# The chunk matrices of a delta-rule recurrence: X read off XT by 128x128 transpositions and half-switching copies, where a third product per chunk made it

## The chip, the cores and the metric

The kernel runs on one core of one Trainium2 chip. The metric is the device time of one execution in microseconds: 4751.49 us is the median of three runs of the kernel before (4750.6 to 4759.0). PE is the matrix engine (TensorE), PEld its weight loads, DVE is VectorE, ACT is ScalarE, POOL is GpSimd, SP issues DMAs.

## What is computed

One launch computes three blocks of two layers each on a sequence of 512 tokens, 1024 wide, in fp32. The change lies in the odd layer of the third block, whose branch C is a recurrence in two directions over 16 heads of width 64:

```python
def wkv7_step(state, inp):
    r, w, k, v, a, b = inp
    sa = jnp.einsum('...ij,...j->...i', state, a)
    state = (state * w[..., None, :] + sa[..., :, None] * b[..., None, :]
             + v[..., :, None] * k[..., None, :])
    y = jnp.einsum('...ij,...j->...i', state, r)
    return state, y
```

with a = -kk and b = kk * a' (kk is the l2-normalised key, a' a gate), r, k, v, w the receptance, key, value and decay. The state of a head is 64x64.

## The kernel before

The function `wkv` (L3398) works in chunks of 64 tokens. A chunk needs the inverse of a unit triangular 64x64 matrix made of products of the a's and b's. X holds that inverse, XT its transpose. They begin as the identity with the first off-diagonal entries put in (L3887 for XT, L3890 for X), and five levels double the size of the diagonal blocks that are inverted (2, 4, 8, 16, 32, then 64 wide). Only XT is needed at the end (`XTC`).

There are 16 steps: 8 pairs of heads times 2 directions (d). A pair of heads lies on the two halves of the 128 partitions, so `heads` (L3524) issues each product twice, 64x64 on the upper and on the lower half; the 8 chunks of the sequence lie side by side in the free dimension. Each fp32 matmul of the code shows as two matmul rows and two weight loads in the trace. Chunks 0 to 3 are half "a" of a level, 4 to 7 half "b".

A level l (L3666 to L3696 on PE) is:
- POOL: C = AS times the mask of the level (L3508), once `t` of the level before is done.
- PE: t = C and XT, per chunk, 16 matmuls, halves a and b (L3673), into bank 0 and 1.
- ACT: T1 = copy of t, half by half (L3783).
- PE: ct = X and T1, 16 matmuls (L3685), into banks 4 and 5. It waits for X of the level before and for T1.
- PE: cx = T1 and X, 16 matmuls (L3694), into banks 2 and 3; not in level 5.
- DVE: XT += ct, half by half (L3906), then X += cx, half by half (L3911).

Beside the matrices of step n, the kernel runs the chain of step p = n - 1: the state passes through the 8 chunks in order, and each level carries one link of it, between t, ct and cx on PE: `ch_g` (8 matmuls, the first four make G), DVE's copy of G (`gk`, L3798), `ch_sa` (2 matmuls), ACT's copy of SA (`san`, L3720), `ch_ys` (8 matmuls), DVE's scaling of the state (`upd`, L3805). Links 0 to 2 stand in the first part of a step, links 3 to 7 in levels 1 to 5. The first step has no chain beside it, and after the last step a chain runs alone.

The order on each engine is the order in which the code is written; nothing schedules it. `rounds` (L3455) writes out the first two and the last three turns and puts the others in a loop of three passes with four steps each. Engines wait on counting semaphores: a `Marks` object gives each engine's steps names ("t1a", "xt1b", "x1a") in the order in which it completes them, and `count(n, name)` is the value to wait for. `K.apart` is a semaphore increment that keeps the waits before and after it apart.

Of the kernel before, what the change touches and what calls it, by code (L numbers as in the profile page):

```python
# [15 lines left out]
P = 128  # L16
# [3381 lines left out]
def wkv(K, base, WDA, W2, RZ, out):  # L3398
# [24 lines left out]
    AS, X, XT, T1, C = (chunks(a) for a in (L, EP, EN, RN, TMP))  # L3423
# [5 lines left out]
    hr = lambda h: slice(64 * h, 64 * h + 64)  # L3429
# [3 lines left out]
    def halves(b):  # L3433

        two = K.psflat[:, b * 512:b * 512 + 1024].rearrange("p (b n) -> p b n", b=2)[:, :, 0:256]
        return two.rearrange("p b (j t) -> p b j t", t=64)
    block_of = lambda b, j: halves(b)[:, j // 4, j % 4, :]
    couple = lambda b: K.psflat[:, b * 512:b * 512 + 1024].rearrange("p (j m t) -> p j m t", m=2, t=64)
    chunks_of = lambda half: range(4) if half == "a" else range(4, 8)
    in_half = lambda a, half: a[:, 0:4, :] if half == "a" else a[:, 4:8, :]  # L3440
    bank_half = lambda b, half: halves(b)[:, "ab".index(half), :, :]
    levels = range(1, 6)

    PM = Marks(K, "wkv_pe", "wa kkn tv tb bon tk sa srb sk " +
               " ".join(f"t{l}a t{l}b ct{l}a ct{l}b" + (f" cx{l}a cx{l}b" if l < 5 else "") for l in levels))
    AM = Marks(K, "wkv_act", "sw aa sqk ln rn ep en eplus ee vt bt kt as " + " ".join(f"t{l}a t{l}b" for l in levels))
    DM = Marks(K, "wkv_dve", "r k v lw scan lprev max kk b bhat a1 kp rk ahat khat rhat bo bo2 xt0 x0 mrb mak mrk " +
               " ".join(f"xt{l}a xt{l}b" + (f" x{l}a x{l}b" if l < 5 else "") for l in levels))
    GM = Marks(K, "wkv_pool", "w2f pr pk pv ix ixt " + " ".join(f"c{l}" for l in levels))

    def chunk(d, j):
# [21 lines left out]
    with nc.Block() as block:  # L3473
# [38 lines left out]
        def _(pe):  # L3512
# [11 lines left out]
            def heads(dst, lhsT, rhs, start=True, stop=True):  # L3524

                for h in range(2):
                    mm = pe.matmul(dst[hr(h)], lhsT[hr(h)], rhs[hr(h)], start=start, stop=stop, skip_group_check=True)  # L3527
                return mm
# [4 lines left out]
            def ch_g(p, pd, j):  # L3533
                if p is None:
                    return
                m = chunk(pd, j)
                if j == 0:
                    pe.wait_ge(DM.sem, DM.count(p, "xt5b"))
                    pe.wait_ge(K.sem("y_sum"), K.count("y_sum", p))
                    K.apart(pe)  # L3540
                    heads(GP, MAK[:, pd, m, :], VT[:, pd, m, :]).then_inc(K.sem("ch_g"), 1)
                else:
                    pe.wait_ge(K.sem("ch_s"), K.count("ch_s", 7 * p + j))
                    K.apart(pe)
                    heads(GP, MAK[:, pd, m, :], VT[:, pd, m, :], stop=False)
                    heads(GP, AR[:, pd, m, 0, :], S, start=False).then_inc(K.sem("ch_g"), 1)
                heads(yp(m), VT[:, pd, m, :], MRK[:, pd, m, :], stop=False)
                if j:
                    heads(yp(m), S, AR[:, pd, m, 1, :], start=False, stop=False)
# [32 lines left out]
            def step(n, d, c, par, p, pd, nth, fin=None):  # L3582
                def projection(half):
                    if nth is None:
                        return
                    q = 1 - par
                    if d == 0 and half == 0:
                        pe.wait_ge(K.landed[(first + q) % 2], 16 * ((first + q) // 2 + 1) + 16 * nth)
                    m = 2 * d + half
                    pe.wait_ge(K.sem("raw_kept"), K.count("raw_kept", 4 * (c + 1) + m - 1))  # L3590
                    pe.wait_ge(DM.sem, DM.count(n - 1, "x4b"))
                    project(q, m)
                if n is not None:
                    pe.wait_ge(GM.sem, GM.count(n, "w2f"))
# [71 lines left out]
                for l in levels:  # L3666
                    if n is not None:
                        pe.wait_ge(GM.sem, GM.count(n, f"c{l}"))
                        for half in "ab":
                            pe.wait_ge(DM.sem, DM.count(n, f"xt{l - 1}{half}" if l > 1 else "x0"))  # L3670
                            K.apart(pe)
                            for j in chunks_of(half):
                                mm = heads(block_of(0, j), C[:, j, :], XT[:, j, :])  # L3673
                            mm.then_inc(PM.step(f"t{l}{half}"), 1)
                    ch_g(p, pd, l + 2)
                    if n is not None:
                        if l == 1:
                            pe.wait_ge(DM.sem, DM.count(n, "mrb"))
                        else:
                            pe.wait_ge(DM.sem, DM.count(n, f"x{l - 1}b"))  # L3680
                        for half in "ab":
                            pe.wait_ge(AM.sem, AM.count(n, f"t{l}{half}"))
                            K.apart(pe)
                            for j in chunks_of(half):
                                mm = heads(block_of(4, j), X[:, j, :], T1[:, j, :])  # L3685
                            mm.then_inc(PM.step(f"ct{l}{half}"), 1)
                    ch_sa(p, pd, l + 2)
                    if n is not None and l < 5:
                        if l == 1:
                            pe.wait_ge(DM.sem, DM.count(n, "mrk"))  # L3690
                            K.apart(pe)
                        for half in "ab":
                            for j in chunks_of(half):
                                mm = heads(block_of(2, j), T1[:, j, :], X[:, j, :])  # L3694
                            mm.then_inc(PM.step(f"cx{l}{half}"), 1)
                    ch_ys(p, pd, l + 2)  # L3696


# [93 lines left out]
        def _(dve):  # L3792
# [31 lines left out]
            def step(n, d, c, par, p, pd, nth, fin=None):  # L3824
# [73 lines left out]
                for l in levels:  # L3898
                    gk(p, pd, l + 2)
                    if n is not None:  # L3900
                        last = f"x{l - 1}b" if l > 1 else "x0"
                        dve.wait_ge(DM.sem, DM.count(n, last))
                        for half in "ab":
                            dve.wait_ge(PM.sem, PM.count(n, f"ct{l}{half}"))
                            x = in_half(XT, half)
                            dve.tensor_tensor(x if l < 5 else in_half(XTC[:, d], half), x, bank_half(4, half), ALU.add)\  # L3906
                               .then_inc(DM.step(f"xt{l}{half}"), 1)
                        for half in "ab" if l < 5 else "":
                            dve.wait_ge(PM.sem, PM.count(n, f"cx{l}{half}"))
                            x = in_half(X, half)  # L3910
                            dve.tensor_tensor(x, x, bank_half(2, half), ALU.add).then_inc(DM.step(f"x{l}{half}"), 1)  # L3911
                    upd(p, pd, l + 2)
                if p is not None:
                    dve.wait_ge(K.sem("ch_ys"), K.count("ch_ys", 8 * p + 8))
# [185 lines left out]
```

## Time and profile before

| | us |
|---|---|
| median of three runs | 4751.49 |
| the profiled execution | 4748.9 |
| its span, first to last instruction | 4746.7 |
| PE busy | 4400.7 (93%) |
| PE weight loads busy | 3338.7 (70%) |
| DVE busy | 2457.6 (52%) |
| ACT busy | 1608.9 (34%) |
| POOL busy | 320.5 (7%) |

The `wkv` function takes from about 3808 to 4650 us of the span. The mean granted clock of PE is 0.960 of full speed. A span is counted from the first instruction, a row's start from the same point. In a timeline row "x128" means that many instructions merged, and the duration is that of the merged run; PE's ends are modelled. The bracket behind a row gives the engine's idle time before it, and what ended it; "issue" stands for nothing that the profile shows.

### The profile page before, as it was taken

How to read it: one execution, taken by the hardware profiler on the slowest of the kernel's cores; microseconds unless marked ns; L12 is line 12 of the kernel's file. 1: busy time of each engine (PE TensorE's matmuls, PEld its weight loads, DVE VectorE, ACT ScalarE, POOL GpSimd, SP SyncE). 2: the span in 40 equal slices, each digit the busy share in tenths (PEclk: the TensorE clock that was granted, in tenths of full speed). 3: DMA queues.
4: the chain of work that ended last, by engine and by line, in shares of the span. 5: the costliest groups of instructions: out<-in, count | busy, mean ns of one | idle time of the engine just before them, and what ended most of it. 6: DMA issues, size and time to landing. Idle time of an engine off the chain costs nothing. (4 is left out here: it accounts for less than half of the span.)

```text
span 4746.7 us, 79005 instructions
## 1 busy us (share of the span) xinstructions
PE 4400.7 (93%) x32172; PEld 3338.7 (70%) x32172; DVE 2457.6 (52%) x3963; ACT 1608.9 (34%) x2467; POOL 320.5 (7%) x307
## 2 busy tenths in 40 slices
PE   8898999899999989999998899978998999999987
PEld 7665788676688767888887644456877567766775
DVE  3634543433445331777777379943534355555553
ACT  2324322323322232666665210133222233334332
POOL 0120000000000000111111000000000022221220
PEclk9888999998999999999999999989998999999998
DMA  3201222221122232111111312111221210000101
GB/s 146 108 19 71 89 89 107 76 89 71 57 104 89 110 129 82 56 59 51 59 54 35 142 53 89 71 54 71 107 98 71 105 37 20 21 20 20 56 3 54
DMA packets 36644, 337.23 MB, mean 71 GB/s; under 512 B 4080, under 2 KB 6384, under 8 KB 18544
## 3 DMA queue, kind: packets, MB, share of 16 engines
q1 hardware_dynamic: 36336, 332.76, 19.0%
q8 instruction: 238, 3.90, 0.3%
q14 instruction: 70, 0.57, 0.0%
HBM read 320.16 MB, written 12.58 MB: 70 GB/s over the span
## 5 line engine op out<-in xcount | busy, mean ns | idle before, releaser
L539 PE MATMUL ps<-hi,weight_parts 128*128 128x512 f32 x5136 | 1611.5, 395 | 120.6 <-DVE lo L406 75.7
L539 PEld LDWEIGHTS ps<-hi,weight_parts 128*128 128x128 f32 x5136 | 979.8, 191 | 340.8 <-issue 122.0
L539 PE MATMUL ps<-lo,weight_parts 128*128 128x512 f32 x2568 | 1011.7, 394 | 0.0
L527 DVE TENSOR_TENSOR weight_parts<-w,weight_parts 128x1024 fp32r<-128x1024 f32 (+1 forms) x336 | 406.8, 1212 | 967.6 <-ACT weight_parts L518 967.5
L518 ACT ACTIVATE weight_parts<-w 128x1024 fp32r<-128x1024 f32 (+1 forms) x336 | 351.7, 1048 | 1197.0 <-PE ps L539 996.1
L539 PEld LDWEIGHTS ps<-lo,weight_parts 128*128 128x128 f32 x2568 | 490.5, 191 | 102.0
L3527 PEld LDWEIGHTS ps<-buffers 64*64 64x64 f32 x12544 | 430.5, 136 | 125.9 <-issue 123.9
L3527 PE MATMUL ps<-buffers 64*64 64x64 f32 x12544 | 460.0, 226 | 52.0 <-issue 27.1
L2409 PE MATMUL ps<-x_parts,column_parts 128*128 128x512 f32 x1536 | 360.7, 392 | 10.5 <-DVE column_parts L2643 9.9
L2884 PE MATMUL ps<-x,w 128*128 128x512 f32 x768 | 331.6, 595 | 6.8 <-PEq L815 6.8
L2409 PEld LDWEIGHTS ps<-x_parts,column_parts 128*128 128x128 f32 x1536 | 286.5, 189 | 69.9 <-DVE column_parts L2643 10.3
L2947 DVE SCALAR_TENSOR_TENSOR buffers<-buffers,vecs 128x392 f32<-128x392 f32 (+14 forms) x480 | 286.8, 678 | 0.0
L2884 PEld LDWEIGHTS ps<-x,w 128*128 128x128 f32 x768 | 146.5, 191 | 191.2 <-issue 191.2
L3520 PE MATMUL ps<-h,w 128*128 128x512 f32 x512 | 228.7, 601 | 1.2 <-PEq L3351 1.2
L3520 PEld LDWEIGHTS ps<-h,w 128*128 128x128 f32 x512 | 96.3, 192 | 117.3 <-issue 115.8
L2434 PE MATMUL ps<-h 128*128 128x128 f32 x1024 | 129.4, 281 | 35.0 <-DVE w L2687 22.3
L2434 PEld LDWEIGHTS ps<-h 128*128 128x128 f32 x1024 | 124.5, 195 | 42.3 <-DVE w L2687 21.9
L3783 ACT ACTIVATE buffers<-ps 128x256 f32<-128x256 f32 x160 | 61.3, 383 | 174.7 <-PE ps L3527 168.9
L3508 POOL TENSOR_TENSOR buffers<-buffers,const 128x512 f32<-128x512 f32 x80 | 101.6, 1270 | 272.2 <-PE ps L3527 200.3
L2643 DVE TENSOR_TENSOR column_parts<-w,column_parts 128x1024 fp32r<-128x1024 f32 x64 | 78.5, 1228 | 58.1 <-ACT column_parts L2515 58.1
L2623 POOL MEMSET w<- 128x1024 f32 x1 | 1.0, 951 | 1542.4 <-POOLq L2130 1542.4
L2409 PE MATMUL ps<-context_parts,column_parts 128*128 128x256 f32 x768 | 104.0, 292 | 0.0
(481 smaller groups left out, 5337.1 us busy)
## 6 DMA issues: line engine op xcount, KB each, us to landing
w<-in_weights SPq DMA_DIRECT2D x126, 2048.0 KB, 7.9
w<-in_wh SPq DMA_DIRECT2D x64, 512.0 KB, 3.6
v_kept<-buffers SPq DMA_DIRECT2D x4, 1024.0 KB, 5.2
buffers<-v_kept SPq DMA_DIRECT2D x16, 256.0 KB, 2.6
h<-x_kept SPq DMA_DIRECT2D x2, 2048.0 KB, 10.5
x<-in_xT SPq DMA_DIRECT2D x4, 512.0 KB, 10.7
x_kept<-h SPq DMA_DIRECT2D x1, 2048.0 KB, 7.0
vc_kept<-x SPq DMA_DIRECT2D x4, 512.0 KB, 2.6
```

What stands on the lines that cost most here:

```text
L518: act.activation(K.parts[:, j % 2, 0, 0:nk, :], part_of(K, slot, j, nk, by_row), ACT.Copy)\
L527: dve.tensor_tensor(K.parts[:, j % 2, 1, 0:nk, :], part_of(K, slot, j, nk, by_row), K.parts[:, j % 2, 0, 0:nk, :].bitcast(F32), ALU.subtra ...
L539: mm = pe.matmul(ps, K.parts[:, j % 2, m, k, :], x[:, k * T:(k + 1) * T], start=(first and k == 0 and n == 0), stop=(last and k == nk - 1 ...
L2409: mm = pe.matmul(o, parts[:, half, w, k, :], src[:, m, k, 0:width], start=(k == 0 and n == 0), stop=(k == 7 and n == 2), skip_group_check= ...
L2434: mm = pe.matmul(bank[:, s], l[:, s], r[:, s], start=True, stop=True)
L2643: dve.tensor_tensor(half[:, 1], weight(name), half[:, 0].bitcast(F32), ALU.subtract).then_inc(DL.step(name), 1)
L2884: mm = pe.matmul(bank(i, j), w[:, k, j * P:(j + 1) * P], K.H[:, k, :], start=(k == 0), stop=(k == 7))
L2947: dve.scalar_tensor_tensor(y, u, w, y, ALU.mult, ALU.add).then_inc(K.sem("tapped"), 1)
L3508: pool.tensor_tensor(C, AS, on_chunks(f"{'clow' if d == 0 else 'cup'}{l}"), ALU.mult).then_inc(GM.step(f"c{l}"), 1)
L3520: mm = pe.matmul(K.ps[:, 2 + m % 2, :], w[:, k, m * P:(m + 1) * P], K.H[:, k, :], start=(k == 0), stop=(k == 7))
L3527: mm = pe.matmul(dst[hr(h)], lhsT[hr(h)], rhs[hr(h)], start=start, stop=stop, skip_group_check=True)
L3783: act.activation(in_half(T1, half), bank_half(0, half), ACT.Copy)\
```

## The change

X of a level is no longer made by the third product and the add. From level 2 on, once t is issued, PE transposes XT as it stands after the level before: four transpositions of 128x128, each over two neighbouring chunks, into banks 2 and 3. What comes out has the head in the free dimension and the chunk's parity on the halves of the partitions, so DVE brings it back with four copies of 64 partitions x 256 elements, each from one half of the partitions to the same or the other half (L3907 of the changed kernel). In level 1, X is x0 as before. ct waits for the fourth copy. The waits for "x4b" become waits for "x4", which is now copied in level 5. Lines behind the added ones have numbers up to nine higher.

```diff
--- before.py
+++ after.py
@@ -3440,12 +3440,13 @@
     in_half = lambda a, half: a[:, 0:4, :] if half == "a" else a[:, 4:8, :]
     bank_half = lambda b, half: halves(b)[:, "ab".index(half), :, :]
     levels = range(1, 6)
+    turned = halves(2).rearrange("p b (i h) t -> p b i h t", h=2)
 
     PM = Marks(K, "wkv_pe", "wa kkn tv tb bon tk sa srb sk " +
-               " ".join(f"t{l}a t{l}b ct{l}a ct{l}b" + (f" cx{l}a cx{l}b" if l < 5 else "") for l in levels))
+               " ".join(f"t{l}a t{l}b " + (f"x{l - 1} " if l > 1 else "") + f"ct{l}a ct{l}b" for l in levels))
     AM = Marks(K, "wkv_act", "sw aa sqk ln rn ep en eplus ee vt bt kt as " + " ".join(f"t{l}a t{l}b" for l in levels))
     DM = Marks(K, "wkv_dve", "r k v lw scan lprev max kk b bhat a1 kp rk ahat khat rhat bo bo2 xt0 x0 mrb mak mrk " +
-               " ".join(f"xt{l}a xt{l}b" + (f" x{l}a x{l}b" if l < 5 else "") for l in levels))
+               " ".join((f"x{l - 1} " if l > 1 else "") + f"xt{l}a xt{l}b" for l in levels))
     GM = Marks(K, "wkv_pool", "w2f pr pk pv ix ixt " + " ".join(f"c{l}" for l in levels))
 
     def chunk(d, j):
@@ -3588,7 +3589,7 @@
                         pe.wait_ge(K.landed[(first + q) % 2], 16 * ((first + q) // 2 + 1) + 16 * nth)
                     m = 2 * d + half
                     pe.wait_ge(K.sem("raw_kept"), K.count("raw_kept", 4 * (c + 1) + m - 1))
-                    pe.wait_ge(DM.sem, DM.count(n - 1, "x4b"))
+                    pe.wait_ge(DM.sem, DM.count(n - 1, "x4"))
                     project(q, m)
                 if n is not None:
                     pe.wait_ge(GM.sem, GM.count(n, "w2f"))
@@ -3672,12 +3673,20 @@
                             for j in chunks_of(half):
                                 mm = heads(block_of(0, j), C[:, j, :], XT[:, j, :])
                             mm.then_inc(PM.step(f"t{l}{half}"), 1)
+                        if l == 2:
+                            pe.wait_ge(DM.sem, DM.count(n, "mrk"))
+                        if l > 1:
+                            K.apart(pe)
+                            for q in range(4):
+                                mm = pe.transpose(K.ps[:, 2 + q // 2, (q % 2) * P:(q % 2 + 1) * P],
+                                                  XT[:, 2 * q:2 * q + 2, :].rearrange("p r t -> p (r t)"), K.c("ident"))
+                            mm.then_inc(PM.step(f"x{l - 1}"), 1)
                     ch_g(p, pd, l + 2)
                     if n is not None:
                         if l == 1:
                             pe.wait_ge(DM.sem, DM.count(n, "mrb"))
                         else:
-                            pe.wait_ge(DM.sem, DM.count(n, f"x{l - 1}b"))
+                            pe.wait_ge(DM.sem, DM.count(n, f"x{l - 1}"))
                         for half in "ab":
                             pe.wait_ge(AM.sem, AM.count(n, f"t{l}{half}"))
                             K.apart(pe)
@@ -3685,14 +3694,6 @@
                                 mm = heads(block_of(4, j), X[:, j, :], T1[:, j, :])
                             mm.then_inc(PM.step(f"ct{l}{half}"), 1)
                     ch_sa(p, pd, l + 2)
-                    if n is not None and l < 5:
-                        if l == 1:
-                            pe.wait_ge(DM.sem, DM.count(n, "mrk"))
-                            K.apart(pe)
-                        for half in "ab":
-                            for j in chunks_of(half):
-                                mm = heads(block_of(2, j), T1[:, j, :], X[:, j, :])
-                            mm.then_inc(PM.step(f"cx{l}{half}"), 1)
                     ch_ys(p, pd, l + 2)
 
 
@@ -3898,17 +3899,20 @@
                 for l in levels:
                     gk(p, pd, l + 2)
                     if n is not None:
-                        last = f"x{l - 1}b" if l > 1 else "x0"
-                        dve.wait_ge(DM.sem, DM.count(n, last))
+                        if l > 1:
+                            dve.wait_ge(PM.sem, PM.count(n, f"x{l - 1}"))
+                            for h in range(2):
+                                for r in range(2):
+                                    to = X[hr(h)].rearrange("p (b i r) t -> p b i r t", b=2, r=2)[:, :, :, r, :]
+                                    ins = dve.tensor_copy(to, turned[hr(r), :, :, h, :])
+                            ins.then_inc(DM.step(f"x{l - 1}"), 1)
+                        else:
+                            dve.wait_ge(DM.sem, DM.count(n, "x0"))
                         for half in "ab":
                             dve.wait_ge(PM.sem, PM.count(n, f"ct{l}{half}"))
                             x = in_half(XT, half)
                             dve.tensor_tensor(x if l < 5 else in_half(XTC[:, d], half), x, bank_half(4, half), ALU.add)\
                                .then_inc(DM.step(f"xt{l}{half}"), 1)
-                        for half in "ab" if l < 5 else "":
-                            dve.wait_ge(PM.sem, PM.count(n, f"cx{l}{half}"))
-                            x = in_half(X, half)
-                            dve.tensor_tensor(x, x, bank_half(2, half), ALU.add).then_inc(DM.step(f"x{l}{half}"), 1)
                     upd(p, pd, l + 2)
                 if p is not None:
                     dve.wait_ge(K.sem("ch_ys"), K.count("ch_ys", 8 * p + 8))
```

On PE, a level of the last step, from the second half of t to the start of `ch_ys`. Before, where L3527 is `heads`, which issues t, `ch_g`, ct, `ch_sa`, cx and `ch_ys`:

```order
L3527 MATMUL ps<-buffers 64x64 [waits wkv_dve]
L3527 MATMUL ps<-buffers 64x64 x7
L3527 MATMUL ps<-buffers 64x64 [waits ch_s]
L3527 MATMUL ps<-buffers 64x64 x7
L3527 MATMUL ps<-buffers 64x64 [waits wkv_dve,wkv_act]
L3527 MATMUL ps<-buffers 64x64 x7
L3527 MATMUL ps<-buffers 64x64 [waits wkv_act]
L3527 MATMUL ps<-buffers 64x64 x7
L3527 MATMUL ps<-buffers 64x64 [waits ch_gk]
L3527 MATMUL ps<-buffers 64x64 x17
L3527 MATMUL ps<-buffers 64x64 [waits ch_san]
```

And now on PE, in level 2, where `heads` is L3528 and the transpositions are L3681:

```order
L3528 MATMUL ps<-buffers 64x64 [waits wkv_dve]
L3528 MATMUL ps<-buffers 64x64 x7
L3681 MATMUL ps<-const,buffers 128x128 [waits wkv_dve]
L3681 MATMUL ps<-const,buffers 128x128 x3
L3528 MATMUL ps<-buffers 64x64 [waits ch_s]
L3528 MATMUL ps<-buffers 64x64 x7
L3528 MATMUL ps<-buffers 64x64 [waits wkv_dve,wkv_act]
L3528 MATMUL ps<-buffers 64x64 x7
L3528 MATMUL ps<-buffers 64x64 [waits wkv_act]
L3528 MATMUL ps<-buffers 64x64 x7
L3528 MATMUL ps<-buffers 64x64 [waits ch_gk]
L3528 MATMUL ps<-buffers 64x64
```

The transpositions stand between t's second half and `ch_g`; of the 17 matmuls behind `ch_sa`'s first, 16 (cx) are gone, so that the wait for `ch_san` follows `ch_sa` directly.

On DVE, a level in the last steps. Before, with the copy of G (L3798), the adds to XT (L3906), the adds to X (L3911) and the scaling of the state (L3805):

```order
L3798 COPY buffers<-ps 128x64 [waits ch_sa,ch_g]
L3906 TENSOR_TENSOR buffers<-buffers,ps 128x256 [waits wkv_pe,wkv_dve]
L3906 TENSOR_TENSOR buffers<-buffers,ps 128x256 [waits wkv_pe]
L3911 TENSOR_TENSOR buffers<-buffers,ps 128x256 [waits wkv_pe] x2
L3805 TENSOR_SCALAR buffers<-ps,buffers 128x64 [waits ch_ys]
```

And now on DVE, with the copies of the turned XT (L3907) and the adds to XT (L3914):

```order
L3799 COPY buffers<-ps 128x64 [waits ch_sa,ch_g]
L3907 COPY buffers<-ps 64x4x64 [waits wkv_pe]
L3907 COPY buffers<-ps 64x4x64 x3
L3914 TENSOR_TENSOR buffers<-buffers,ps 128x256 [waits wkv_pe] x2
L3806 TENSOR_SCALAR buffers<-ps,buffers 128x64 [waits ch_ys]
```

The copies stand behind the copy of G and ahead of the adds to XT; only the first of them waits.

## Rows read from the trace of the kernel before

**Rows 1.** Groups by line and shape, 3822 to 4700 us (busy us, mean ns | idle).
```profile
L3527 PE MATMUL ps<-buffers 64*64 64x64 f32 x11520 | 408.3, 222 | 52.0 <-issue 27.1 <-DVE buffers L3805 13.6 <-ACT buffers L3720 9.3
...
L3911 DVE TENSOR_TENSOR buffers<-buffers,ps 128x256 f32<-128x256 f32 x128 | 53.9, 421 | 19.0 <-PE ps L3527 16.0
```

**Rows 2.** Timeline (start, us, engine, line), a level of the last step.
```profile
4601.92 0.82 DVE L3906 TENSOR_TENSOR buffers<-buffers,ps 128x256 f32<-128x256 f32 x2 [0.54 <-PE ps L3527]
...
4603.37 3.97 PE L3527 MATMUL ps<-buffers 64*64 64x64 f32 x128
...
4604.30 0.85 ACT L3783 ACTIVATE buffers<-ps 128x256 f32<-128x256 f32 x2 [1.64 <-PE ps L3527]
4604.81 1.27 POOL L3508 TENSOR_TENSOR buffers<-buffers,const 128x512 f32<-128x512 f32 x1 [2.58 <-PE ps L3527]
4605.00 0.23 DVE L3798 COPY buffers<-ps 128x64 f32<-128x64 f32 x1 [1.00 <-PE ps L3527]
4605.77 0.82 DVE L3906 TENSOR_TENSOR buffers<-buffers,ps 128x256 f32<-128x256 f32 x2 [0.54 <-PE ps L3527]
4606.28 0.22 ACT L3720 ACTIVATE buffers<-ps 128x64 f32<-128x64 f32 x1 [1.13 <-PE ps L3527]
```

**Rows 3.** Timeline of PE alone, levels 3 to 5 of the seventh step.
```profile
4147.72 3.00 PE L3527 MATMUL ps<-buffers 64*64 64x64 f32 x89 [0.58 <-issue]
4150.53 0.31 PE L3527 MATMUL ps<-buffers,const 64*64 64x64 f32 x4
4150.64 0.98 PE L3527 MATMUL ps<-buffers 64*64 64x64 f32 x27
4152.23 3.13 PE L3527 MATMUL ps<-buffers 64*64 64x64 f32 x101 [0.61 <-issue]
...
4156.79 2.43 PE L3527 MATMUL ps<-buffers 64*64 64x64 f32 x75 [0.79 <-issue]
```

**Rows 4.** Timeline of all engines, the end of the last step's level 5.
```profile
4614.51 0.22 ACT L3720 ACTIVATE buffers<-ps 128x64 f32<-128x64 f32 x1 [1.13 <-PE ps L3527]
...
4614.88 0.33 PE L3527 MATMUL ps<-buffers 64*64 64x64 f32 x4 [0.42 <-ACT buffers L3720]
```

**Rows 5.** Timeline, first adds to XT: levels 1 and 5, seventh and last step.
```profile
4140.45 0.89 DVE L3906 TENSOR_TENSOR buffers<-buffers,ps 128x256 f32<-128x256 f32 x2 [0.48 <-PE ps L3527]
...
4158.67 0.89 DVE L3906 TENSOR_TENSOR buffers<-buffers,ps 128x256 f32<-128x256 f32 x2 [0.47 <-PE ps L3527]
...
4598.07 0.81 DVE L3906 TENSOR_TENSOR buffers<-buffers,ps 128x256 f32<-128x256 f32 x2 [0.55 <-PE ps L3527]
...
4614.00 0.82 DVE L3906 TENSOR_TENSOR buffers<-buffers,ps 128x256 f32<-128x256 f32 x2 [0.55 <-PE ps L3527]
```

**Rows 6.** Timeline, first adds to XT in levels 1 and 5 of the first step.
```profile
3834.92 0.86 DVE L3906 TENSOR_TENSOR buffers<-buffers,ps 128x256 f32<-128x256 f32 x2 [0.34 <-PE ps L3527]
...
3847.53 0.82 DVE L3906 TENSOR_TENSOR buffers<-buffers,ps 128x256 f32<-128x256 f32 x2 [1.48 <-PE ps L3527]
```

**Rows 7.** Timeline of PE, a group of fp32 transpositions in the recurrence of another stage.
```profile
2231.47 0.60 PE L2453 MATMUL ps<-const,h 128*128 128x128 f32 x4
```

**Rows 8.** Timeline of DVE, around the start of the seventh step.
```profile
4103.94 0.69 DVE L3916 COPY buffers<-ps 128x512 f32<-128x512 f32 x1 [0.43 <-PE ps L3527]
...
4109.89 2.07 DVE L3831 SCALAR_TENSOR_TENSOR buffers<-buffers,vecs 128x511 f32<-128x511 f32 x3
...
4121.48 0.75 DVE L3852 SCALAR_TENSOR_TENSOR buffers<-buffers,vecs 128x512 f32<-128x512 f32 x1 [0.74 <-ACT buffers L3757]
...
4122.26 0.69 DVE L3854 TENSOR_TENSOR buffers<-buffers 128x512 f32<-128x512 f32 x1
```

**Rows 9.** Stretches: us, busy of PE PEld DVE ACT POOL, PEclk, DMA share, GB/s.
```profile
222.00:225.00 3.00, 1.70 (x47) 1.38 (x48) 0.63 (x2) 2.17 (x2) 0.00 (x0) 1.00 0.03 5
...
4618.00:4620.00 2.00, 1.10 (x23) 0.80 (x20) 0.51 (x2) 0.22 (x1) 0.00 (x0) 1.00 0.00 0
4620.00:4622.00 2.00, 1.71 (x27) 1.58 (x29) 0.28 (x1) 0.00 (x0) 0.00 (x0) 0.50 0.00 0
```

## The prediction

> **What bounds the kernel now.** I began with the two lines of the page on the span and on the engines' busy shares: PE is busy for 93% of the 4746.7 us, but that is a mean over twelve stages, so I went to the stage that holds the change, the `wkv` function, which runs from about 3808 to 4650 us. Grouped by line, its largest entry is the helper `heads`: 11520 matmul rows of 64x64 there [rows 1], two rows for each matmul in the code (16 matmuls in `t`, 32 rows). The DVE adds that finish X are 128, of 0.42 us [rows 1].
>
> Next I read the timeline of one level that nothing disturbs, in the last of the 16 steps [rows 2]. The reader is to see that PE's row goes on for 128 matmul rows without a gap: ACT, POOL and DVE each wake, work and sleep beside it, and PE waits for none of them. Counting from the code, a level of a step with a chain has 32 rows of t, 16 of `ch_g`, 32 of ct, 4 of `ch_sa`, 32 of cx and 16 of `ch_ys`: 132. The first add to XT stands at 4601.92 and at 4605.77 in two levels running ([rows 2]), so a level takes 3.85 us, and a row 3.85 / 132 = 0.0292 us. Level boundaries: t begins at 4603.37 + 8 x 0.0292 = 4603.60, since eight rows of `ch_ys` stand in front of it in that group.
>
> From the same rows come the delays from PE's issue of the last row to the start of the engine that waited: 16 rows of t are out at 0.47 us, ACT begins at 4604.30 - 4603.60 = 0.70, so 0.23; `ch_g`'s first eight rows are out at 40 x 0.0292 = 1.17, DVE's copy begins at 1.40, again 0.23; ct's first half is out at 1.87, the add begins at 2.17, so 0.30. Back to PE it is 0.15: ACT ends at 4614.73, PE starts at 4614.88 [rows 4].
>
> Third, the same levels in the middle of the stage. They are longer than 3.85, and the gaps carry "issue", not a partner [rows 3]. They stand at no wait of the code: between the gap before the 89 rows and the one before the 101 rows lie 89 + 4 + 27 = 120 matmul rows, with as many weight loads, so some 250 instructions with the waits and register writes. I read them as PE running out of fetched instructions. From the first add of level 1 to that of level 5 the seventh step takes 18.22 us and the last one 15.93 [rows 5]; the mean of the 15 steps with a chain is 17.45, against 4 x 3.85 = 15.40 without gaps: 2.05 us a step.
>
> So PE's own rows bound the levels, with fetching on top, and everything else has room. The change takes rows from PE and puts a round trip through DVE on its path.
>
> **Part by part.** (1) Removed on PE: 32 rows of cx in levels 1 to 4, and 32 x 0.0292 = 0.93 us each. (2) Removed on DVE: two adds of 0.42 us a level [rows 1], which no one waited for before ct of the next level. (3) Added on PE: four 128x128 fp32 transpositions in levels 2 to 5. A group of four took 0.60 us with a row of 0.27 [rows 7], so (0.60 - 0.27) / 3 = 0.11 each, 0.44 for four at the full clock. (4) Added on DVE: four copies of 64 partitions x 256 elements from PSUM. None is in the trace. A copy from PSUM took 0.69 us for 512 elements and 0.23 for 64 [rows 2, 8], so 0.425 for 256 by the straight line between them; fewer partitions I take to save nothing.
>
> How closely four copies follow each other is open. Three DVE operations without a wait between them took 2.07 us; one of this form and size lasts 0.75, so they started (2.07 - 0.75) / 2 = 0.66 apart, 0.09 less than one lasts; where one waited for the one before, it started 0.03 after its end (4121.48 + 0.75 to 4122.26) [rows 8]. By the first, four copies take 3 x 0.34 + 0.43 = 1.45 us, by the second 4 x 0.425 + 3 x 0.035 = 1.81. I take 1.81, because these copies change the half of the partitions each time, in source or destination, which the three operations did not.
>
> The Trainium skill (VectorE: DVE Perf Modes, Two Vector instructions with no wait between them) says that an instruction whose first input or output starts in another quadrant than the one before it is held until all earlier ones have finished; all four copies would be. By that rule the 1.81 holds, without it the 1.45; no row of this trace shows a change of half.
>
> (5) The new wait. PE's order in a level is t, transpositions, `ch_g`, then ct, which waits for X. DVE's order is its copy of G first, which waits for `ch_g`, then the four copies. So the cover for the round trip is `ch_g` alone, 0.47 us. For a step with a chain, from the start of t: t out at 0.93, transpositions 1.37, the first half of `ch_g` 1.60, DVE's copy of G from 1.83 to 2.06, the four copies from 2.09 to 3.90, PE again at 4.05. Before, ct began at 48 x 0.0292 = 1.40. Then ct 0.93 (4.98), `ch_sa` 0.12 (5.10). Behind it stands the second loss: `ch_ys` waits for ACT's copy of SA, which cx used to cover: 5.10 + 0.23 + 0.22 + 0.15 = 5.70. `ch_ys` 0.47 ends the level at 6.17. Queued behind the waiting ct is all of PE's stream; no other engine has work that could use the time. The adds to XT (first at 4.05 + 0.47 + 0.30 = 4.82, second over by 5.7) and POOL's product (1.27 us from the end of t, [rows 2]) are done by then.
>
> The sum for such a step: levels 2, 3 and 4 go from 3.85 to 6.17, +2.32 each. Level 5 had no cx before, so it was 84 x 0.0292 + 0.60 + 0.47 = 3.52: +2.65. Level 1 loses cx and has no transpositions: 3.52 for 3.85, -0.33. Together 6.96 + 2.65 - 0.33 = +9.28. Of the fetching gaps I count all 2.05 as gone: a level has now 32 + 4 + 16 + 32 + 4 + 16 = 104 matmul rows for 6.17 us where it had 132 for 3.85, and a fetch has the waits to catch up in. Net +7.2, for 15 steps +108.
>
> The first step has no chain. Its levels took 12.61 / 4 = 3.15 us [rows 6]. Now: t 0.93, transpositions 1.37, copies 1.60 to 3.41, ct from 3.56, its first half out at 4.03, the add 4.33 to 4.75, next t at 4.90: +1.75 in three levels, some +2.3 in level 5, -0.6 in level 1: +7.
>
> What the gaps are worth: if they stay, 31 us more. The Trainium skill (Runtime: NRT & Kernel Launch, Instruction fetch mechanics) has the instructions come in blocks of 256 and the crossing "mostly hidden". The number agrees with the 120 matmul pairs, the "hidden" does not: 0.58, 0.61 and 0.79 us [rows 3]. By the page fewer instructions would give nothing back, and the sum would be 31 us higher.
>
> The total is +115 on the profiled execution's own 4748.9 us, which lies 2.6 below the median of the three runs: 4864 us. With copies that overlap (-0.36 in 64 levels, -23) it is 4841; with the gaps left in (+31) 4895.
>
> **Rivals.** (a) Forecast: levels of about 6.2 us, clock mostly at its upper level, 4864. Its own range is 4830 to 4900. Chance 0.72.
>
> (b) The clock falls inside the levels. PE now stands idle for about 2.2 us and 0.6 us in each 6.17. The trace has both answers: in the last chain, with PE rows in 1.10 of 2 us, the granted clock went from 1.00 to 0.50 (2.4 to 1.2 GHz), while an earlier stage, busy for 1.70 of 3 us, kept 1.00 [rows 9]. The new levels lie between. At half clock their rows cost 100 x 0.0292 + 0.44 = 3.4 us more a level; were it so for half of the 64 levels with transpositions, +109: about 4973, and 4918 if for a quarter of them. Chance 0.22. The Trainium skill (TensorE: Matmul & The Clock Gate, Part 4: PE-mode transpose) says that transpositions do not count as busy for the clock gate, which speaks for this rival; here they are only 0.44 of 3.4 us of work, and the transpositions of [rows 7] stand among ordinary matmuls, so nothing in the trace tests it.
>
> (c) Faster. If X came back before PE needs it, ct would not wait. A level 2, 3 or 4 would then take 3.52 + 0.44 = 3.96 for 3.85, since cx also covered the wait for SA; level 5 +0.44, level 1 -0.33: +0.44 a step, with the gaps -2.05 it is -1.6, 15 x 1.6 = 24 us less: 4725. It decides in ct's wait: from the transpositions to a copied X no more than the 0.47 us of `ch_g` may pass, in place of 2.5 us. Copies several times cheaper than 0.425 would do it; ACT's T1, there at 0.70 + 0.85 = 1.55 after the start of t, would not stand in the way. Chance 0.04.
>
> (d) Between (a) and (c): X comes some 0.4 us a level late, and the gaps that go pay for it: 4749, within 0.2%. Chance 0.02.
>
> **How the numbers follow.** What the measurement of this kernel can tell from no change is about 0.2%, 10 us. Faster 0.04, same 0.02, slower 0.94. The range takes in all of (a) and the lower part of (b): 4820 to 4930.
>
> **What would show it.** Right: PE idle of about 2.2 us before ct in levels 2 to 5, released by the last DVE copy; four copies in about 1.8 us, starting behind the copy of G; PE idle of 0.4 us before `ch_ys`, released by ACT; first adds to XT 6.2 us apart; the "issue" gaps gone from the levels; transpositions 0.11 us apart. Wrong: T1 or the second add to XT named as what PE waits for; copies of under 0.3 us; a granted clock under 0.9 over the levels, which makes it (b).

## The result and the profile after

The changed kernel took 4952.0 us (median of 4 runs, 4932.2 to 4965.1) against 4755.2 us (4 runs, 4750.6 to 4760.0): a ratio of 1.041, 95% interval 1.040 to 1.043. It is 197 us slower, where the prediction had +115 and a range up to 4930. The direction was right, the size was not. Its profiled execution took 4965.1 us (span 4962.9).

First the groups by line and shape of the changed kernel, 3822 to 4900 us, which answer to [rows 1]:

```profile
L3528 PE MATMUL ps<-buffers 64*64 64x64 f32 x9472 | 443.5, 248 | 172.3 <-DVE buffers L3907 122.2 <-ACT buffers L3721 33.7 <-DVE buffers L3806 14.3
...
L3907 DVE COPY buffers<-ps 64x256 f32<-64x256 f32 x256 | 107.4, 419 | 12.6 <-PE ps L3681 10.0
```

L3528 is `heads`. The matmul rows fell from 11520 to 9472, as counted, and "issue" is no longer among the three reasons named: in the levels of the 15 steps with a chain not one gap of that kind is left, as forecast. In the whole stretch `heads` still has 5.4 us of it in 3 gaps, 4.3 of them in one that the kernel before has too. In place of the gaps PE waits 122.2 us in 64 times (1.91 each) for the last copy of X, and for ACT's copy of SA 33.7 us instead of 9.3. But two things stand here that the sum did not have. The waits grew by less than the time did, and one 64x64 row lasts 248 ns on average where it lasted 222.

A level that nothing disturbs (the changed kernel's timeline, all engines but the weight loads; it answers to [rows 2]):

```profile
4099.98 0.89 DVE L3914 TENSOR_TENSOR buffers<-buffers,ps 128x256 f32<-128x256 f32 x2 [0.96 <-PE ps L3528]
...
4101.18 1.36 PE L3528 MATMUL ps<-buffers 64*64 64x64 f32 x40
...
4102.11 0.85 ACT L3784 ACTIVATE buffers<-ps 128x256 f32<-128x256 f32 x2 [1.33 <-PE ps L3528]
4102.47 0.66 PE L3681 MATMUL ps<-const,buffers 128*128 128x128 f32 x4
...
4103.06 0.68 PE L3528 MATMUL ps<-buffers 64*64 64x64 f32 x16
4103.56 0.23 DVE L3799 COPY buffers<-ps 128x64 f32<-128x64 f32 x1 [1.74 <-PE ps L3528]
4103.70 1.72 DVE L3907 COPY buffers<-ps 64x256 f32<-64x256 f32 x4
4105.65 1.26 PE L3528 MATMUL ps<-buffers 64*64 64x64 f32 x36 [1.91 <-DVE buffers L3907]
4106.37 0.89 DVE L3914 TENSOR_TENSOR buffers<-buffers,ps 128x256 f32<-128x256 f32 x2 [0.96 <-PE ps L3528]
4106.95 0.22 ACT L3721 ACTIVATE buffers<-ps 128x64 f32<-128x64 f32 x1 [3.99 <-PE ps L3528]
4107.32 0.33 PE L3528 MATMUL ps<-buffers 64*64 64x64 f32 x4 [0.41 <-ACT buffers L3721]
```

The chain is the one forecast, link by link: transpositions, half of `ch_g`, DVE's copy of G, four copies, ct, `ch_sa`, ACT's copy of SA, `ch_ys`. The first adds to XT of two levels running stand at 4099.98 and 4106.37: 6.39 us for a level, where 6.17 was forecast.

Most levels are longer than that. Of the 60 periods from one first add to XT to the next (levels 1 to 5, the 15 steps with a chain) only 16 are under 6.55 us, and 22 are over 8.0. The reader sees why in the levels at 4162 to 4178: PE's rows of the timeline, then the stretches (us, busy of PE PEld DVE ACT POOL, granted clock, DMA share, GB/s), which answer to [rows 9].

```profile
4162.23 1.43 PE L3528 MATMUL ps<-buffers 64*64 64x64 f32 x40
4163.59 0.66 PE L3681 MATMUL ps<-const,buffers 128*128 128x128 f32 x4
...
4166.77 2.26 PE L3528 MATMUL ps<-buffers 64*64 64x64 f32 x36 [1.91 <-DVE buffers L3907]
...
4169.88 2.38 PE L3528 MATMUL ps<-buffers 64*64 64x64 f32 x40
4172.19 1.11 PE L3681 MATMUL ps<-const,buffers 128*128 128x128 f32 x4
```

```profile
4163.00:4166.00 3.00, 1.85 (x43) 1.48 (x38) 1.30 (x4) 0.77 (x2) 1.26 (x1) 1.00 0.01 3
4166.00:4169.00 3.00, 2.23 (x36) 2.10 (x36) 1.09 (x4) 0.00 (x0) 0.00 (x0) 0.62 0.00 0
4169.00:4172.00 3.00, 2.60 (x49) 2.60 (x48) 0.55 (x2) 0.61 (x2) 0.00 (x0) 0.50 0.02 5
```

The same 40 rows take 1.43 us and then 2.38, 36 rows 1.26 and 2.26, with the granted clock at 1.00 and then at 0.50, the 1.2 GHz level. The fall comes as PE takes up its work behind the wait of 1.91 us. So it is nearly everywhere: over the 16 steps the granted clock falls to 0.50 44 times, for 266 us in all, and 42 of these falls begin between 0.3 us before and 2.0 us after PE starts again behind a wait for X; in the kernel before it falls 4 times, for 24 us. Over a long part of the stage (before, then after; the same columns) the clock reads:

```profile
3826.00:4600.00 774.00, 715.26 (x14243) 543.55 (x14241) 419.93 (x887) 288.73 (x565) 169.09 (x169) 0.98 0.07 24
```

```profile
3826.00:4600.00 774.00, 640.23 (x9712) 466.57 (x9708) 361.84 (x777) 222.90 (x436) 132.19 (x132) 0.87 0.05 18
```

So the theory was: the round trip costs about what was forecast, and the waits it makes let the clock fall, rival (b), on top. The rival theory: the long levels have another cause, the transpositions or the copies themselves.

### The profile page after: what moved, and what is told of

The parts are those of the page before. It is cut to its first block and busy times, and to the rows that moved or that the text cites. A ratio compares the mean times of both kernels' runs of the same rounds, so it can differ in the third digit from the quotient of the medians.

```text
span 4962.9 us, 75485 instructions
## 1 busy us (share of the span) xinstructions
PE 4495.1 (91%) x30380; PEld 3392.4 (68%) x30380; DVE 2511.5 (51%) x4091; ACT 1609.7 (32%) x2467; POOL 320.2 (6%) x307
## 5 line engine op out<-in xcount | busy, mean ns | idle before, releaser
L3528 PE MATMUL ps<-buffers 64*64 64x64 f32 (+1 forms) x10496 | 494.3, 250 | 172.3 <-DVE buffers L3907 122.2
L3528 PEld LDWEIGHTS ps<-buffers 64*64 64x64 f32 x10496 | 444.4, 156 | 276.5 <-issue 275.1
L3721 ACT ACTIVATE buffers<-ps 128x64 f32<-128x64 f32 x128 | 28.5, 223 | 412.7 <-PE ps L3528 412.7
L3799 DVE COPY buffers<-ps 128x64 f32<-128x64 f32 x128 | 28.8, 225 | 199.7 <-PE ps L3528 199.7
L3914 DVE TENSOR_TENSOR buffers<-buffers,ps 128x256 f32<-128x256 f32 x160 | 67.3, 421 | 96.7 <-PE ps L3528 94.6
```

## The experiments

Kernels in one block of runs share the runs of the kernel before (4757.5, 4752.8 and 4752.1 us in the three blocks, 4755.2 in that of the result), so differences between blocks are good to a few us. A level, in this section, is the period between first adds to XT, "undisturbed" its commonest value.

**Filling the wait.** Four matmuls that nobody reads go behind `ch_g` in levels 2 to 5:

```diff
                     ch_g(p, pd, l + 2)
+                    if n is not None and l > 1:
+                        for q in range(4):
+                            pe.matmul(K.ps[:, 5, 256:512], K.c("ident"), K.const[:, 0:256], start=True, stop=True)
```

> The changed kernel with four extra 128x128x256 matmuls per level 2 to 5, whose results nothing reads, put into TensorE's wait for the copies of X (about 1.7 us of work in a wait of 1.91 us). Theory A (the clock falls because of the wait): of 60 level-to-level periods of the changed kernel 22 were over 8.0 us where a warm one is 6.4, and the granted clock over the steps was .87 against .98 before. If the wait is what lets it fall, it now stays up, nearly all periods are 6.4 to 6.6, the clock of the steps is near .97, and the time is about 4952 - 64 x 1.2 = 4875 (4860 to 4895). Theory B (the long levels have another cause: the four transpositions, the copies or the semaphores themselves): the clock stays low, the fillers only lengthen the levels in which TensorE is slow, 4950 to 5010.

Measured: 4878.9 us (4877.1 to 4879.8), 73 less than the changed kernel, by adding work. Ratio to before 1.026 (1.024 to 1.027). The clock and a level of the last step:

```profile
3826.00:4600.00 774.00, 725.21 (x10932) 523.26 (x10930) 397.03 (x850) 248.10 (x482) 141.77 (x141) 0.99 0.05 19
```

```profile
4731.72 0.89 DVE L3917 TENSOR_TENSOR buffers<-buffers,ps 128x256 f32<-128x256 f32 x2 [0.91 <-PE ps L3528]
...
4735.42 1.99 PE L3687 MATMUL ps<-const 128*128 128x256 f32 x8
4735.44 1.72 DVE L3910 COPY buffers<-ps 64x256 f32<-64x256 f32 x4
4737.34 1.26 PE L3528 MATMUL ps<-buffers 64*64 64x64 f32 x36
4738.07 0.89 DVE L3917 TENSOR_TENSOR buffers<-buffers,ps 128x256 f32<-128x256 f32 x2 [0.91 <-PE ps L3528]
```

PE's matmuls (L3687) lie beside DVE's copies and ct starts as before; the level is 6.35 to 6.40, and 58 of the 60 periods are under 6.55, where 16 were. Transpositions and copies are all still there. That fells the other theory and splits the loss: 121 us for all that the change does at the full clock (transpositions, copies and waits, less the removed rows and gaps), 73 for the clock.

**One matmul instead of four**, the same edit with `range(1)`.

> The changed kernel with one extra 128x128x256 matmul per level 2 to 5 in the wait for the copies, instead of four (.43 of work in 1.91 of wait, against 1.7). With four the time fell from 4952 to 4879 and 58 of 60 periods were under 6.6. If it is the length of the idle stretch that lets the clock fall, and little work doesn't mend that, most of the loss stays: 4930 to 4950. If any work inside the wait does: 4879 as with four. If the share of busy time decides, between them by the quarter of the work: about 4930.

Measured: 4891.4 us (4887.5 to 4896.8), granted clock 0.98, close to the fill with four; "by the quarter of the work", 4930, is excluded. PE's waits for X in the same stretch (line waited for: us, times, longest), of the changed kernel and of this one:

```profile
PE ps L3528 <- DVE buffers L3907: 92.4, 48, 2.2
```

```profile
PE ps L3528 <- DVE buffers L3910: 61.4, 51, 1.5
```

**The copies of X ahead of the copy of G** on DVE:

```diff
-                    gk(p, pd, l + 2)
+                    if n is None or l == 1:
+                        gk(p, pd, l + 2)
...
                             ins.then_inc(DM.step(f"x{l - 1}"), 1)
+                            gk(p, pd, l + 2)
```

> The changed kernel with VectorE doing the four copies of X before the copy of G in levels 2 to 5. The copies wait for the transpositions (end at .66 after their start), the copy of G comes after ch_g, so the copies start about .45 us earlier and TensorE is released .45 earlier; the copy of G, which ch_ys needs two groups later, is then late by 1.3 us but still ahead of ct's end. Theory A (the round trip is the term, its wait shortens from 1.91 to 1.46): warm level 5.95 instead of 6.4, 64 x .45 = 29 us less, 4923. Theory B (the wait is also what lets the clock fall, and a shorter one lets it fall less often): 4870 to 4915, with fewer periods over 8 us than the 22 of 60.

Measured: 4863.1 us (4860.6 to 4872.8), below both expectations. The undisturbed level is 5.88, so 0.52 shorter, and 12 of 60 periods are over 7.1. Clock 0.95; the waits for X are 73.1 us in 52 (1.41 each). With this the runs form a row: mean waits of 1.93, 1.41 and 1.20 us (the last with one matmul in it) and next to none (0.6 us in 3, with four) went with clocks of 0.87, 0.95, 0.98 and 0.99. Half a microsecond on DVE was worth 89 us in all, 0.52 x 64 = 33 of it directly; the other 56 came with the higher clock.

**The price of the transpositions.** The kernel before with four of them a level into unused halves of banks, and with two:

```diff
+                        if l > 1:
+                            for q in range(4):
+                                pe.transpose(K.ps[:, 4 + q // 2, 256 + (q % 2) * P:256 + (q % 2 + 1) * P],
+                                             XT[:, 2 * q:2 * q + 2, :].rearrange("p r t -> p (r t)"), K.c("ident"))
```

> The kernel before with the four transpositions of a level added (levels 2 to 5), into halves of banks that nothing reads: the price of the transpositions alone on TensorE, with no new wait. Theory A (they cost what the changed kernel shows between the last matmul of t and the first of ch_g, .59 us, and keep the clock as it was): 64 x .59 = 38 us, 4793. By the .11 each of the prediction: 64 x .44 = 28 us, 4783. Theory B (transpositions themselves lower the clock): well over that, 4830 or more, with a granted clock under .95 over the steps.

> The kernel before with two transpositions of 128x128 a level (levels 2 to 5) that nothing uses, where the run with four made an undisturbed level 4.58 instead of 3.85 (.73, not the .44 of the prediction). If each costs what its start in the trace says (.165 from one to the next, .66 for four less the last one's tail) and the rest is a fixed price of going from the 64x64 products to a 128x128 one and back: .73 - 2 x .147 = .44 for two, a level of 4.29 and 4757 + 64 x .44 + some 5 of fetched instructions = 4790. Rival: no fixed price, each costs .18: .37 for two, 4.22, 4785. Rival: the transpositions are cheap and the going over is all: 4.5 or more for two as well, 4805.

Measured: 4809.1 us with four (ratio 1.011, 1.009 to 1.013) and 4796.6 with two (1.009, 1.008 to 1.011). PE in an undisturbed level, with four and with two:

```profile
4656.84 1.36 PE L3527 MATMUL ps<-buffers 64*64 64x64 f32 x40
...
4658.13 0.66 PE L3677 MATMUL ps<-const,buffers 128*128 128x128 f32 x4
...
4658.72 2.78 PE L3527 MATMUL ps<-buffers 64*64 64x64 f32 x88
```

```profile
4648.98 1.33 PE L3527 MATMUL ps<-buffers 64*64 64x64 f32 x40
...
4650.25 0.44 PE L3677 MATMUL ps<-const,buffers 128*128 128x128 f32 x2
...
4650.62 2.78 PE L3527 MATMUL ps<-buffers 64*64 64x64 f32 x88
```

A level takes 3.85 us with none, 4.37 with two, 4.58 with four: (4.58 - 4.37) / 2 = 0.105 for each, and 0.52 - 0.21 = 0.31 that comes with the first ones and not with more of them, which I put down to going over from 64x64 products to 128x128 ones and back. That the price is a straight line with such a foot rests on three levels; one or three transpositions were not run. The 0.11 of the prediction was right and the fixed 0.31 was missing; my expectation for two had it too small. The granted clock stayed at 0.99 and 0.98, so transpositions without a wait do not lower it. Of the 52 us with four, 0.73 x 64 = 47 are this price, of the 45 with two (4796.6 against 4752.1) 0.52 x 64 = 33. The rest is in the gaps with "issue", which grew to 38.2 us in the stretch in both, from 28.5. The gaps are also what makes 35 of the 60 periods with four longer than 5.2 us: 34 of them lie in these levels, 31.8 us in all.

**The removed part alone.** The kernel before without cx and without the additions to X; X is not updated and ct no longer waits for it, so this part of the computation is left out.

```diff
-                    if n is not None and l < 5:
...
-                                mm = heads(block_of(2, j), T1[:, j, :], X[:, j, :])
-                            mm.then_inc(PM.step(f"cx{l}{half}"), 1)
```

> The kernel before without the third product of each chunk and the additions to X (X stays what it was at a step's start, so what the levels compute is not the reference's): the removed part of the change alone, with nothing in its place. By the terms of the prediction: level 1 to 4 lose .33 us each (of .93 of removed matmuls .60 comes back as the wait for SA that they covered), and the fetch gaps 2.05 us a step: 16 x (4 x .33 + 2.05) = 54 us, about 4701 (4680 to 4715). Rival: the removed matmuls were also what kept TensorE's clock up, the clock falls in the levels and the time is 4760 or more. The level-to-level time on a warm clock would be 3.85 - .33 = 3.5 us.

Measured: 4746.1 us (10 runs, 4739.5 to 4754.7), ratio 0.998 (0.997 to 0.999): 11 us and not 54, with the clock at 0.98, so neither expectation held. The undisturbed level is 3.54, as worked out. But PE's waits (3826 to 4600 us) of this kernel, and then of the kernel before, show where it went:

```profile
PE ps L3527 <- issue: 43.8, 55, 4.2
PE ps L3527 <- ACT buffers L3712: 23.6, 58, 0.4
```

```profile
PE ps L3527 <- issue: 28.5, 37, 4.3
PE ps L3527 <- DVE buffers L3805: 11.9, 29, 0.9
PE ps L3596 <- issue: 7.0, 2, 3.6
PE ps L3527 <- ACT buffers L3720: 5.7, 14, 0.4
```

The wait for SA came as forecast (+18), and the fetch gaps did not go, they grew. Of the 15 us more under "issue" 5 are 15 gaps of 0.36 us, each ending 0.10 us behind ACT's copy of SA, so waits for it; 10 remain. The undisturbed levels save 64 x 0.31 = 20 us, and the gaps take about half of it back. With 2048 of the 11520 rows gone PE gets through the rest sooner, and stands without instructions for longer.

That these gaps are fetching, which I had argued from the counts of rows, can be read in the trace. The profile has a DMA queue that it calls "instruction"; in the kernel before, between 3826 and 4600 us (packets, MB, share of 16 engines' span):

```profile
q8 instruction: 120, 1.97, 1.0%
```

These are packets of 16 KB. The three gaps of [rows 3] end at 4147.72, 4152.23 and 4156.79, and a packet had landed at 4146.38, 4150.80 and 4155.43. It is so for every "issue" gap in the 60 levels of the kernel before: 32 gaps over 0.15 us, 19.0 us in all, each ending 1.2 to 1.6 us after a packet's landing, while only about one moment in ten of these levels lies so behind one. 63 packets came for these levels, one for 125 matmul rows, so half of them show a gap. In the changed kernel 60 packets came for the same levels, and none shows one. The gap of 4.3 us follows no packet; its cause is open.

**Taking the round trip off the path, step by step.** First the transpositions go ahead of t, so that t and `ch_g` cover the copies (with the copies ahead of that of G):

```diff
+                            pe.wait_ge(DM.sem, DM.count(n, f"xt{l - 1}b"))
                             K.apart(pe)
                             for q in range(4):
...
+                        pe.wait_ge(GM.sem, GM.count(n, f"c{l}"))
+                        for half in "ab":
...
+                            mm.then_inc(PM.step(f"t{l}{half}"), 1)
```

> The changed kernel with VectorE's copies ahead of its copy of G (as in the run before) and with the four transpositions moved ahead of t at a level's start, so that TensorE has the eight-chunk product t and ch_g to do while VectorE copies. Theory (the round trip and the clock that falls in it are the loss): TensorE's wait for the copies shrinks from 1.46 to about .3, a warm level is 4.75 instead of 5.88, 64 x 1.13 = 72 us less than 4863, 4790 (4775 to 4815), with the clock no lower than in the kernel before. Rival (the transpositions themselves let the clock fall: with them alone in the kernel before, 35 of 60 periods were over 5.2 where a warm one is 4.58): about half the levels are at 6.0, 4830.

Measured: 4799.3 us (4796.8 to 4805.6), ratio 1.010 (1.008 to 1.012); level 4.95, clock 0.98, the waits for X are down to 25.4 us in 54. The theory held within 0.2 us a level (4.75 forecast), and the loss fell from 197 to 47 us.

Then two of the four copies go to ACT:

```diff
+                            act.wait_ge(PM.sem, PM.count(n, f"x{l - 1}"))
+                            for h in range(2):
+                                ins = act.activation(x_place(h, 0), turned[hr(0), :, :, h, :], ACT.Copy)
```

> The kernel of the run before (transpositions ahead of t), with two of the four copies of X on ScalarE instead of VectorE (it does them while t is computed, ahead of its copies of t). Theory: X is ready about .8 us earlier than with four on VectorE, TensorE's own work and ScalarE's copies of t become the bound, a warm level of 4.1 instead of 4.75, 64 x .65 = 42 us less, 4750 (4735 to 4790). Rival: ScalarE, now two copies later with t, is the wait: the level stays at 4.6 to 4.75, 4790.

Measured: 4778.7 us (4770.2 to 4781.9), ratio 1.005 (1.004 to 1.007), level 4.29, no wait for X left. Half of the expected 42 us came: the level fell by 0.66, as expected, and the gaps took the rest. ACT is not the wait of the rival (0.7 us in 3); "issue" rose from 8.4 to 21.3 us.

Last, `ch_sa` goes between the halves of ct:

```diff
                             mm.then_inc(PM.step(f"ct{l}{half}"), 1)
-                    ch_sa(p, pd, l + 2)
+                            if half == "a":
+                                ch_sa(p, pd, l + 2)
```

> The kernel with shared copies and with ch_sa between the two halves of ct, so that ScalarE's copy of SA lies under ct's second half and ch_ys has not to wait for it. Theory: the wait for SA (.41 a level in the changed kernel, 33.7 us in 83 waits over the steps) goes: 64 x .4 = 26 us less than with shared copies alone, 4725 (4705 to 4765), under the kernel before, whose wait for fetched instructions (31.6 us in 41) these kernels don't have. Rival: ch_sa, between the halves, makes the second half of ct and with it the additions to XT later by what it saves: 4750, as the kernel before.

Measured: 4756.4 us (10 runs, 4753.3 to 4759.6), ratio 1.0006 (0.9996 to 1.0016): the kernel before's time, so the kernel before is not beaten. Its waits (3800 to 4700 us) and a level:

```profile
PE ps L3529 <- issue: 42.9, 43, 4.3
PE ps L3529 <- DVE buffers L3816: 15.4, 36, 1.4
```

```profile
4610.03 0.63 PE L3676 MATMUL ps<-const,buffers 128*128 128x128 f32 x4
4610.59 3.25 PE L3529 MATMUL ps<-buffers 64*64 64x64 f32 x88
4610.70 0.77 ACT L3790 ACTIVATE buffers<-ps 64x256 f32<-64x256 f32 x2 [1.47 <-PE ps L3676]
4610.70 0.87 DVE L3916 COPY buffers<-ps 64x256 f32<-64x256 f32 x2 [0.45 <-PE ps L3676]
```

The wait for SA is down to 3.2 us in 8, PE's rows close up to 88 in one group, the undisturbed level is 3.85, the very length of [rows 2]. With PE's waits gone the fetch gaps are back at 38.5 us in 40 (3826 to 4600), so the theory's 4725, which had counted them out, fell.

## Why the prediction was wrong

The step that failed is in the sum of part (5): all of PE's rows behind the new waits were priced at the full clock, so that the clock stood at nothing in the 4864. The runs give 73 us for it. The second miss is a size, part (3): 0.44 us for transpositions that cost 0.73. With that alone mended the sum would have been near the 4879 of the fill run, inside the range.

- **Removed rows, part (1) and (2):** the count and the 0.0292 us a row held (level 3.54 without cx, 3.52 forecast).
- **Transpositions, part (3):** the step that was mis-sized in the level. 0.105 each, as read, and a fixed 0.31 for changing between the shapes that [rows 7] could not show, since no 64x64 products stand beside that group: 0.73 a level for 0.44.
- **Copies, part (4):** four took 1.72 us, 0.43 from start to start, near the 1.81 and far from the 1.45. The rule of the Trainium skill cited there (VectorE: DVE Perf Modes) agrees with the trace: behind the copy of G, which starts at the same partition, the first copy even began 0.09 us before its end (4103.56 + 0.23 against 4103.70), but from one half to the other each waited for the one before. So three of the four were held, where the prediction had all four. Four copies without a change of half were not run.
- **The new waits, part (5):** right, both of them. PE idle 1.91 us (2.2 forecast, the ends of matmul rows being counted as busy) and 0.41 for SA (0.60 forecast, for the same reason). 6.17 + 0.31 - 0.09 = 6.39, the level measured: the two differences are those of parts (3) and (4). Over 64 levels these two add 14 us to the 4864; the fill run, with the clock up, gave 4879.
- **The fetch gaps:** gone from the levels, as forecast, and for the reason given last, the waits. Fewer rows alone do not do it, as the run without cx shows. The mean of the 15 steps is 17.51 us and not 17.45, 1 us in all, and 19.0 of the 32 us by which their levels exceed 3.85 lie in the gaps themselves. The Trainium skill says of the crossing from one block of instructions to the next that it is "mostly hidden" (Runtime: NRT & Kernel Launch, Instruction fetch mechanics). In the levels of the kernel before the trace does not agree, with gaps at 32 of 63 packets; in the changed kernel, where PE has its waits, it does, with none at 60.
- **The first step:** +13.4 us for the +7 forecast (12.61 to 25.98); with the wait filled, three of its four levels take 4.93 to 5.02, where 4.9 was forecast, and the fourth 9.86, with an "issue" gap of 2.35 us and the lower clock behind it. The changed kernel has such a gap there too, 2.13 us beside its waits of 1.91, and its clock stays at 0.50 from 3845.85 on for 20 us. So of the 6 us that were not forecast about 2 are a fetch gap and the rest is the clock.
- **The clock, where the prediction failed:** 73 us. It was rival (b), with the right mechanism and a price for a quarter of the levels (54 us) and a half (109) between which the 73 lie, but a chance of 0.22. The forecast added up a level as if each had PE's full clock, though it had just put 2.8 us of waiting into every 6.2. [Rows 9] showed both answers; I said that the new levels lie between, and gave the answer of the busier stretch 0.72, although the other one was of this very stage. Of the 82 us by which the profiled steps exceed those of the fill run, 57 lie in the levels, 24 between level 5 and the next level 1: a step's next part starts at the low clock too. (The 82 are of the profiled executions; that of the changed kernel, 4965.1, is the slowest of its four.) The Trainium skill says that the gate does not count transpositions as busy in the same way (TensorE: Matmul & The Clock Gate, Part 4: PE-mode transpose), which would help the clock to fall. No run here shows it: in the kernel before, with no wait added, they left it at 0.99, and in the fill run too.
- **Rival (c), faster at 4725:** its condition, X back before ct needs it, was built with the shared copies, and gave 4779. The level is 4.29 there and not 3.96, by the dearer transpositions, and of the gaps, counted as gone, 12.1 us in 16 are back in the levels. With the wait for SA covered too it is 4756: the gaps, 20.0 us in 25 in the levels, come back as PE's waits go.

## What to carry to other kernels

Where a change puts a wait of microseconds into every round of a loop that TensorE fills, price the rounds at both clock levels and take the forecast from the lower one as seriously as the upper; the test is to fill the wait with matmuls that nobody reads. Moving work off TensorE through another engine can pay only if the way back is covered: half a microsecond less of a wait was worth 89 us here. That was not enough to gain: with the cover complete the time was that of the kernel before. In a stage of small matmuls the supply of instructions can be a bound of its own; here removing 2048 of 11520 rows gave back 0.2%, the rest going to a wait that they had covered and to longer gaps.

## What the runs showed of the hardware

- Extra matmuls made the kernel 73 us faster: granted clock 0.87 to 0.99, and one matmul of 0.43 us a level gave some 60 of the 73.
- The granted clock fell around the end of waits of PE of 1.8 to 2.3 us, 42 times in 16 steps.
- Two and four 128x128 fp32 transpositions between 64x64 products cost 0.52 and 0.73 us: 0.105 each and 0.31 besides.
- "issue" gaps on PE depend on its other waits: 28.5 us before, 43.8 with fewer matmuls (5 of them waits for SA), none in the changed kernel's `heads` (3826 to 4600 us), 8.4, 21.3 and 38.5 as its waits were taken away.
- Each "issue" gap in the levels of the kernel before ended 1.2 to 1.6 us after a 16 KB packet of the instruction queue had landed (32 of 32). So did those of the last two kernels, 1.2 to 1.7 us (12.1 us in 16 and 20.0 in 25).
- These gaps are about two thirds of what lies between the 4.29 or 3.85 us of the last two kernels and their means (18.45 / 4 = 4.61, 17.44 / 4 = 4.36). The last third was not traced, and no run changed the number of instructions at equal work.
